# Second block by token tiles: tile 0's attention, projections and first PEER head ahead, tile 1's behind them

## The reference, cut to what matters

```
h = modulate(x, norm1_g, sh1, sc1)
x = x + g1 * token_mixer(h)
x = x + g2 * peer(modulate(x, norm2_g, sh2, sc2))

token_mixer:  z = h @ w_in + b_in
  y_hy = hyena(z_hy) @ w_hy_out
  y_na = attend(q, k, v, k_ctx, v_ctx) @ w_na_out   # 8 heads of 64; local scores + bias, context scores
  gate = sigmoid(z_gates)
  return (gate[:D] * y_hy + gate[D:] * y_na) @ w_out

peer (per token): 8 heads; q @ keys -> 2 x 128 scores, top 16 of each, top 16 of the 256 sums,
  idx = 16 experts, g = softmax(best);  out = sum_k g_k * gelu(x . u[idx_k]) * v[idx_k]
```

## Time and profile before

| | us |
|---|---|
| median of 3 runs | 2703.54 (2703.3 to 2706.32) |
| the profiled execution | 2704.44 |
| its span, first to last instruction | 2702.5 |
| PE busy | 2506.6 (93%) |
| DVE busy | 2072.8 (77%) |
| ACT busy | 1257.6 (47%) |
| POOL busy | 271.6 (10%) |
| HBM read | 821.34 MB, 304 GB/s over the span |
| q0, the indirect DMAs | 268.45 MB |

### The profile page before, as it was taken

One profiled execution on the slowest core, in us unless ns is written; L12 is line 12 of the kernel. 1 busy time (PEld: TensorE's weight loads), 2 busy tenths in 40 slices (PEclk: granted clock), 3 DMA queues, 4 the chain that ended last, 5 costly groups with the idle time before them and its releaser, 6 DMA issues. The chain is left out here.

```text
span 2702.5 us, 37397 instructions
## 1 busy us (share of the span) xinstructions
PE 2506.6 (93%) x14282; PEld 2161.1 (80%) x14282; DVE 2072.8 (77%) x3104; ACT 1257.6 (47%) x1540; POOL 271.6 (10%) x290
## 2 busy tenths in 40 slices
PE   5999999999999999999999999989998998778787
PEld 4789997787888888888888877747777898777786
DVE  6778984767898989899898974635748878887875
ACT  3234443236777777677777763103422333323322
POOL 0000001000000000000000000000003444333331
PEclk9999999989999999999999998999989999999999
DMA  8647675557999999999999956211558999999997
GB/s 350 245 176 285 273 286 199 216 197 286 354 356 355 356 346 344 355 353 356 353 358 354 355 190 240 114 42 67 212 236 347 412 421 420 420 421 421 421 421 298
DMA packets 109273, 824.90 MB, mean 305 GB/s; under 512 B 11864, under 2 KB 15192, under 8 KB 16096
## 3 DMA queue, kind: packets, MB, share of 16 engines
q1 hardware_dynamic: 71504, 551.75, 53.5%
q0 software_dynamic: 36864, 268.45, 24.0%
...
HBM read 821.34 MB, written 1.05 MB: 304 GB/s over the span
## 5 line engine op out<-in xcount | busy, mean ns | idle before, releaser
L1682 DVE TENSOR_TENSOR ring_r<-ring,arena_r 128x2048 fp32r<-128x2048 f32 x336 | 770.2, 2292 | 11.5
L2064 ACT ACTIVATE arena_r<-ring 128x2048 fp32r<-128x2048 f32 x378 | 725.6, 1920 | 29.0 <-DMA ring<-in_ffn_w_down 14.4
L634 PE MATMUL ps<-arena_r 128*128 128x512 f32 (+1 forms) x1120 | 417.2, 373 | 1.5 <-DVE arena_r L1718 1.5
L636 PE MATMUL ps<-arena_r 128*128 128x512 f32 x896 | 349.3, 390 | 0.0
L635 PE MATMUL ps<-ring_r,arena_r 128*128 128x512 f32 x896 | 348.6, 389 | 0.0
L1344 PE MATMUL ps<-sel,ring 128*128 128x128 f32 x2096 | 267.9, 285 | 59.7 <-ACT sel L2064 58.5
L1344 PEld LDWEIGHTS ps<-sel,ring 128*128 128x128 f32 x2096 | 251.9, 198 | 73.8 <-ACT sel L2064 71.5
L2064 ACT ACTIVATE sel<-cs,arena 128x128 f32<-128x128 f32 x256 | 102.8, 402 | 420.8 <-DVE arena L2022 381.5
L1344 PE MATMUL ps<-sel,arena 128*128 128x128 f32 x2000 | 249.5, 281 | 43.8 <-ACT sel L2064 38.1
L1344 PEld LDWEIGHTS ps<-sel,arena 128*128 128x128 f32 x2000 | 236.4, 195 | 55.3 <-ACT sel L2064 48.4
L634 PEld LDWEIGHTS ps<-arena_r 128*128 128x128 f32 x1120 | 211.3, 189 | 35.6 <-DVE arena_r L1718 1.8
...
## 6 DMA issues: line engine op xcount, KB each, us to landing
...
```

The source lines that it names most:

```text
L634: e.matmul(out, xs[0], ws[0], start=start, stop=False, skip_group_check=True)
L636: return e.matmul(out, xs[1], ws[0], start=False, stop=stop, skip_group_check=True)
L1682: v(e.tensor_tensor(ring_low[ring.half[unit]], ring.buf[unit], mo.high[unit_at[unit] % NHIGH].bitcast(F32), ALU.subtract), ("low", unit))
L2064: A.mark(e.activation(out, src, func, **kw), name)
```

## The change

1. Two of the eight ada2 tiles move out of the second block into the expert stage: four half loads and eight dots, at units 18, 19, 25, 26, 32, 33, 39 and 40.
2. The zero-padded copies of k go. `scores` handles two heads at once, each over its 64 rows (rows 0 to 63 and 64 to 127), product by product in turn, into four score banks.
3. The 16 iterations run over tile 0's eight heads, then tile 1's. A whole w_in2 part (3584, second half) stands before the first scores. Behind tile 0's heads lie w_in2 4096, w_hy and w_in2 4608; behind tile 1's heads tile 0's w_na (`na(0)`) and w_out2 (`out2(0)`), its residual (`added`) and the squares of its norm. The sigmoid becomes (1 + tanh(x/2)) / 2 in four pieces (`gate_tanh`), with the half taken in the residual's factor.
4. After the loop tile 1's `na(1)` stands around the spread of tile 0's norm; six of the eight steps of `out2(1)` come after the first two heads' scores, the last two before rows 1 and 3. Tile 1's residual, norm sums, root, spread and scaling lie between rows 3 and 17.
5. PEER's queries and scores are for one tile and one head each (`HEADS`, `ASKED`), every 16 rows over both tiles.
6. There are 7 row buffers up to row 123, 9 from 124, 11 from 152, 13 from 184. The buffer of row 6 waits for `("mix2", 1, 1)`, the last step of `out2(1)`.
7. Loads: bias in two halves, w_in2 4096 ahead of w_hy, keys in the half slot of the first bias half behind w_pq 0. w_pq 2 and 3 use the slots of w_out2, which are free when `out2(1)` is through with them.

```diff
-    turn, had, out = deque(range(NOWN + 2)), {}, []
-    joins = {24: (NOWN + 2, NOWN + 3), 58: (NOWN + 4, NOWN + 5), 92: (NOWN + 6, NOWN + 7),
-             96: (NOWN + 8, NOWN + 9)}
+    turn, had, out = deque(range(NOWN)), {}, []
+    joins = {124: (NOWN, NOWN + 1), 152: (NOWN + 2, NOWN + 3), 184: (NOWN + 4, NOWN + 5)}
     for i in range(256):
...
+NROWS = NOWN + 6
...
+HEADS = [(t, h) for t in range(2) for h in range(8)]
...
+    at = {2: 5, 10: 114, **{j: 16 * j - 38 for j in range(3, 16) if j != 10}}
+    asked = {r + d: (j, q) for j, r in at.items() for q, d in enumerate((0, 2 if j == 2 else 3))}
+    queried = {r + (3 if j == 2 else 4): j for j, r in at.items()}
+    scored = {r + (5 if j == 2 else 6): j for j, r in at.items()}
...
+        ada2 += [Ada("ada2", T["w_ada"], n, [accb], "silu c2 again", "b_ada", [m2[:, 0, :]],
+                     selb if n < 10 else waste) for n in range(4, 12)]
+        behind = {"mix0": ada0[4:10], "mix1": ada1[6:12], "second": ada2[4:10]}
+        behind["moe"] = [t.by_halves() for t in ada2[10:12]]
...
+            m.own = [arena[:, a:a + 2048] for a in (16666, 0, 2048, 14618, 4096, 12570, 10522)]
...
+                used = (P["w_na", 1, 1] if b == 4 else V["merged2", 1, 1] if b == 5 else P["mix2", 1, 1] if b == 6
+                        else P["attended", 15])
...
-            s = ring.slot["w_pq", n] if n < 4 else ring.slot["keys"]
-            used = P["pq", 2 * n + 1] if n < 4 else P["pscore", 7]
-            return slots[s][:, 2048 * h:2048 * h + 2048], P["rows", had] if had is not None else used
+            s = ring.slot["w_pq", n]
+            return (slots[s][:, 2048 * h:2048 * h + 2048],
+                    P["rows", had] if had is not None else P["pq", 1, 2 * n + 1])
...
+                    if turn == 0 and w == "md" and h and i in (17, 24, 31, 38):
+                        load_half(*hidden.pop(0))
...
+                load_half(("bias", t), T["bias"][:, 2048 * t:2048 * t + 2048])
...
             hidden = behind["second"]
             for t in hidden[0:2]:
                 load_ada(t)
+            load(("w_in2", 4096), T["w_in2"][8])
             for n in range(2):
                 load_half(("w_hy", n), T["w_hy"][n])
-            load(("w_in2", 4096), T["w_in2"][8])
             for t in hidden[2:4]:
                 load_ada(t)
             load(("w_in2", 4608), T["w_in2"][9])
-            for t in hidden[4:8]:
+            for t in hidden[4:6]:
                 load_ada(t)
             for n in range(2):
                 load_half(("w_na", n), T["w_na"][n])
-            at = ring.n // 2 % (NSLOT - 1)
-            ring.order, ring.n = ring.order[at:] + ring.order[:at] + [kept], 0
             for n in range(2):
                 load(("w_out2", n), T["w_out2"][n])
-            for n in range(4):
+            load(("w_pq", 0), T["w_pq"][0])
+            rest = ring.order, ring.n
+            ring.order, ring.n = [kept], 0
+            load_half("keys", T["keysT"])
+            ring.order, ring.n = rest
+            for n in range(1, 4):
                 load(("w_pq", n), T["w_pq"][n])
-            load("keys", T["keysT"])
 
...
-            pieces = [piece(c0, i, 2, hT, "hT x") for c0, i in ((3072, 0), (3072, 1), (3584, 0))]
-            pieces.append(branch("w_hy", m.zc, 0, 0))
-            pieces.append(piece(3584, 1, 2, hT, "hT x"))
-            pieces += [branch("w_hy", m.zc, n, p) for n, p in ((0, 1), (1, 0), (1, 1))]
-            pieces += [piece(c0, i, 2, hT, "hT x") for c0 in (4096, 4608) for i in range(2)]
+            pieces = [piece(c0, i, 2, hT, "hT x") for c0 in (3072, 3584) for i in range(2)]
+            behind_heads = [piece(4096, i, 2, hT, "hT x", ASIDE[2:]) for i in range(2)]
+            behind_heads += [branch("w_hy", m.zc, i // 2, i % 2, ASIDE[2:]) for i in range(4)]
+            behind_heads += [piece(4608, i, 2, hT, "hT x", ASIDE[2:]) for i in range(2)]
...
             def scores(i):
-                h, t = its[i]
-                b = bank(("score", i))
-                q = m.qn[:, h // 2, 128 * t:128 * t + 128]
-                e.matmul(b[:, 0:256], q, m.kp[:, h, :], start=True, stop=True)
-                P.mark(e.matmul(b[:, 256:512], q, m.kcp[:, h, :], start=True, stop=True), ("score", i))
-            e.wait_ge(*V["kp"])
-            e.wait_ge(*A["kcp"])
-            for i in range(3):
+                at = []
+                for j in (i, i + 1):
+                    h, t = its[j]
+                    r = slice(64 * (h % 2), 64 * (h % 2) + 64)
+                    at.append((bank(("score", j), SCORES), r, h // 2, t))
+                for c, k in ((0, m.kn), (256, m.kc)):
+                    for j, (b, r, p, t) in enumerate(at):
+                        last = e.matmul(b[:, c:c + 256], m.qn[r, p, 128 * t:128 * t + 128], k[r, p, :],
+                                        start=True, stop=True)
+                        if c:
+                            P.mark(last, ("score", i + j))
+            e.wait_ge(*V["roped", "k"])
+            e.wait_ge(*V["normed", "kc"])
+            def na(t):
...
+            first = chain.from_iterable(behind_heads)
+            second = chain(na(0), out2(0))
+            for i in range(0, 4, 2):
                 scores(i)
             for i, (h, t) in enumerate(its):
-                if i == 0:
-                    next(halves)
-                b = bank(("turn", i))
+                b = bank(("turn", i), (4,))
                 e.wait_ge(*V["scaled", i])
                 P.mark(turned(b, [m.pt[i % 2][:, 128 * k:128 * k + 128] for k in range(4)]), ("turn", i))
-                if i + 3 < len(its):
+                if i % 2 and i + 3 < len(its):
                     scores(i + 3)
-                next(halves, None)
-                if 3 <= i < 5:
-                    next(halves, None)
-                b = bank(("attended", i))
+                next(second if t else first, None)
+                if i == 15:
+                    peer_sums(0)
+                b = bank(("attended", i // 2), (5,)) if i % 2 == 0 else ps.bank["attended", i // 2]
                 e.wait_ge(*A["turn", i])
                 r = slice(64 * (h % 2), 64 * (h % 2) + 64)
                 P.mark(summed(b[r, 0:128], [(m.vs[k][:, 64 * h:64 * h + 64], m.pt[i % 2][:, 128 * k:128 * k + 128])
                                               for k in range(4)]), ("attended", i))
-            for _ in halves:
-                pass
-            e.wait_ge(*A["attended", 15])
-            for n in range(2):
-                for p in range(2):
-                    for _ in branch("w_na", m.yna, n, p):
-                        pass
-            for n in range(2):
-                arrived(("w_out2", n))
-                proj(cols_of(("w_out2", n)), 0, 4, m.gate, ("mix2", n), pairs=None if n else "merged2")
-                done(("w_out2", n))
+                next(second if t else first, None)
             m = pr
             P.stage("peer")
-            norm_sums("norm_peer", range(8))
-            spread("norm_peer")
-
-            def query(h, i):
-
...
+            late = chain(na(1), out2(1))
+            for _ in range(2):
+                next(late)
+            peer_spread(0)
+            for _ in range(2):
+                next(late)
...
+            for j in range(2):
+                for q in range(2):
+                    query(j, q)
+                key_scores(j)
+                if j == 0:
+                    tokens(0)
+            for _ in range(6):
+                next(late)
             for i in range(256):
                 t = i // 128
                 if i % 128 == 0:
                     for q in range(2):
                         bank(("peer", t, q), (2 * t + q,))
-                if i in QUARTERS:
-                    query(*QUARTERS[i])
+                if i in (1, 3):
+                    next(late)
+                if i == 8:
+                    peer_sums(1)
+                if i == 13:
+                    peer_spread(1)
+                if i in ASKED:
+                    query(*ASKED[i])
                 if i in SCORED:
                     key_scores(SCORED[i])
-                    if SCORED[i] == 7:
-                        done("keys")
-                        tokens(1)
...
+            def na(t):
+                c = slice(128 * t, 128 * t + 128)
+                for n in range(2):
+                    if t == n == 0:
+                        arrived(("w_na", 0))
+                        arrived(("w_na", 1))
+                    tile = rows_of(("w_na", n), 4, 512)
+                    b = bank(("w_na", t, n), ASIDE[2:])
+                    if n == 0:
+                        e.wait_ge(*A["attended", 8 * t + 7])
+                    for j in range(4):
+                        s = slice(128 * j, 128 * j + 128)
+                        last = summed(b[:, s], [(tile[:, k, s], se2.yna[:, k, c]) for k in range(4)])
+                        if j == 3:
+                            P.mark(last, ("w_na", t, n))
```

(68 more changed lines are left out.)

301 lines of the change are left out of this document (167 added, 134 removed).

## The result

| | before | after |
|---|---|---|
| time, median (4 runs each) | 2703.42 us | 2743.31 us |
| range of the runs | 2701.45 to 2706.32 | 2738.02 to 2744.96 |
| ratio, 95% interval | | 1.0146 [1.0133, 1.0158] |
| profiled execution, its span | 2704.44, 2702.5 | 2744.96, 2742.7 |

The change makes the kernel 1.5% slower, 40 us. Forecast were 2700 us and a range of 2684 to 2718. The balance of the two profiled executions closes, to a few tenths, on three places: the expert stage ends 13.0 us later, the way from there to the first gather is 16.0 us shorter, and from row 0's dot to row 255's it takes 695.3 us instead of 651.8, 43.5 more: 13.0 - 16.0 + 43.5 = 40.5, and the two executions differ by 40.5.

A forecast was written before the change was run, and what follows sets the result against it. PEER was taken as bound by DMA, the stretch ahead of it by the order of work. First gather -26, start +14.6 - 3.5, thin buffers +12 gave -3 us on 2703.54: 2700 us, range 2684 to 2718.

The forecast's parts named there:

- Part 1: Expert stage: eight ada2 dots and four 1 MB loads move in at cost 0, 10 us at most.
- Parts 2 to 4: From the experts to the last attended product's copy: first turn at 1884.3, tile 1's first turn 1945, copy at 1984.5.
- 1884.3 + 2 + 59: Sum for tile 1's first turn, 1945: tile 0's first turn, 2 us, and eight iterations of tile 0's heads.
- Part 5: From the last attended product's copy to the first gather, forecast at 2008, 26 us earlier than before.
- Part 6: Start of PEER's gathers: row 6 waits for tile 1's last w_out2 product; cost 14.6 us, against 3.5 lost before.
- Part 7: Seven buffers until row 124: 1 us lost in each of 6 heads, some 6 at rows 12-27; 12 together.
- the second rival: PEER: seven buffers starve the queue in every head, 3.4 us in each of 7 heads, 2713 to 2719; chance 0.18.
- The one that ended on the slower side: PEER: same as the second rival, with ScalarE's wait for TensorE's key scores holding up all coefficients; chance 0.18.
- Wrong if the expert stage ends later: Expert stage: a sign listed to refute the forecast, beside DMA at 1.01 from row 8 or first gather outside 2000-2016.
- 14.6 - 3.5 + 12: PEER's terms: 14.6 us for the gathers' start, less 3.5 already lost there, plus 12 for thin buffers.

The follow-up runs named there:

- e1: The changed kernel with both dots of each hidden ada2 half in one unit of the experts: 2727.13 us.
- e11: Changed kernel with dots together, nine buffers, tile 0's norm in bank 0, queries two rows earlier, eight w_out2 steps before row 0, late w_pq tiles held: 2695.10 us.
- e2: The changed kernel with nine row buffers from the start instead of seven: 2718.32 us.
- e10: The changed kernel with the loads of w_pq's third and fourth tiles held until the dots of rows 8 and 24: 2734.26 us.
- e13: e11 with tile 1's norm 32 rows later: 2690.84 us.
- e7: The changed kernel with the queries of heads 3 to 15 asked of TensorE two rows earlier: 2731.86 us.

## Why the prediction was wrong

- **Part 1 failed: 0, with 10 us as the outer bound; it was 13.0.** I asked whether each engine had time for eight dots, and they had. I wrote that loads run several units ahead in a ring of ten halves; at six halves a unit the ring holds less than two. So I didn't ask how long a hidden half keeps its place in it. The loads pass through the ring in order; between a half's two dots lie 19.4 us, and the load that takes its place lands 5 us after the second dot. e1 gives all of it back. "No gain is possible, 10 at most" was a bound on work, and a held buffer isn't work.
- **Parts 2 to 4 held**, within 1.2, 1.1 and 1.9 us. A pair of heads' scores takes 1.07 us where two heads took 1.74 before: 0.53 a head, between my bounds of 0.44 (taken) and 0.87. Inside a pair two instructions take the time of one, 0.215 us. The steps at both changes of form are 0.1 us longer each, the 0.20 us by which the pair misses half; what takes that time the trace doesn't show. Tanh and exp shared one table load (1.28 us at 1891.02, none before the first exp at 1896.73), as I had taken them. The 2 us in 1884.3 + 2 + 59 were my estimate, and no run shows them as a term by themselves. What the kernel after shows in their place: behind the pause of 6.63 us the first turn's four instructions took 1.08 us and the 16 of w_in2 behind them 5.51, at a granted clock of 0.63 from 1898 to 1905 us, where the next 16, at 1.00, took 3.72 and the next turn 0.60: 2.3 us more.
- **Part 5 failed by 5.6 us**: 29.1 from the copy of the last attended product to the first gather, not 23.5. Its terms had no bank and no slow clock. The second half of w_na waits 3.19 us for the norm's bank; the first half is 1.6 to 1.7 us slow in every kernel of the new order, the second 1.7 in this profile too. In e11, with another bank, the way takes 23.9. With the 4.2 us of parts 2 to 4, that is 9.8 of the 10.0 us by which the gain of the first gather fell short (16.0 instead of 26). Some of it belongs to this one execution: in the five other kernels that are the same up to here the gain, counted from the end of the experts, is 17.4 to 21.5 us, still short by 4.5 at least.
- **Part 6: right in its events, wrong in what they cost.** Row 6 was issued at 23.0 us after row 0's dot (forecast: last step near 20). I priced the empty queue at 6 us less 1.4 and the moved w_pq at 10 of traffic, 11 us more than before, and put 6 on VectorE for rows 12 to 27; row 32's dot is 27.9 late. The empty queue was sized about right (e2: 6 to 8). The moved w_pq costs 7.6 at row 32 (e10), but not as traffic: e10 moves the same bytes a little later. It costs because it makes row 1 late, and with it VectorE's and TensorE's row work. Tile 1's norm between rows 3 and 17 costs 7.4 at row 32 (e13, measured on e11), of which 5.1 are left at row 255. The step that failed is the bound: I added up the queue's time, but at row 16 the dot stands 11 us behind its landing. From row 6 to row 16 VectorE is the slower one, and what counts is when its row work gets going and what stands between the rows. The three prices come from different kernels and give 21 to 23 of the 27.9; the rest stays open.
- **Part 7: the right mechanism, too small.** I took one turnover, 11.4 us at row 105, against the 11.6 allowed, and gave 1 us to each of six heads. Rows 32 to 112 took 215.3 us where 204 is what eight or nine buffers need: 2.2 us a head for five heads, halfway between my 1 and the second rival's 3.4. A turnover at one row says nothing of a loop in which VectorE is slower than DMA for half of each head (in e7, 3.1 us a row in rows 36 to 43 against 2.545 a transfer).
- **The rivals.** The one that ended on the slower side (buffers starve, 2713 to 2719) named what happened in PEER, but with the start and the experts each priced too low its time was 24 to 30 us short; its cause, ScalarE waiting for TensorE, was there (5.08 us) and e7 shows that it isn't what costs the later heads. "Wrong if the expert stage ends later" stood in the text as a sign, and no chance was set on it.

The misses add up: 13.0 (experts), 10.0 (first gather), and in PEER 43.5 instead of the 23.1 of 14.6 - 3.5 + 12, which is 20.4 more. Together 43.4: the forecast change of -2.9 against the +40.5 between the two profiled executions.
